# Last projection tile computed in two column halves, first loads cut in half, last row factor by Ln and Exp

## The reference

```
def rmsnorm(x, g):
    y = xf * lax.rsqrt(jnp.mean(xf * xf, axis=-1, keepdims=True) + RMS_EPS)
    return (y * g.astype(jnp.float32)).astype(x.dtype)

h = x
for layer in range(2):
    xn = rmsnorm(h, norm_mix_g[layer])
    # layer 0: xn @ w_in (1024 x 2048), S5 and mLSTM groups, @ w_out
    # layer 1: xn @ w_qkv, windowed attention, @ w_o
    h = h + mix
    # gated MLP: up (1024 x 5632), conv of width 3, silu, times value, down (2816 x 1024)
    h = h + conv_gated_mlp(rmsnorm(h, norm_ffn_g[layer]), ...)
return rmsnorm(h, norm_final_g)
```

## Time and profile before

| | us |
|---|---|
| median of 3 runs | 1170.82 |
| lowest, highest | 1168.13, 1171.21 |
| profiled execution, its own time | 1169.44 |
| profiled execution, span from first to last instruction | 1167.6 |
| PE busy in the span | 1108.7 (95%) |
| DVE, ACT, POOL busy | 666.2, 460.8, 200.6 |
| mean granted TensorE clock | 0.976 |

### The profile page before, as it was taken

The page is one execution under the profiler, slowest core; times in us unless marked ns, Lnnn a source line. Parts: engine busy times, 40 slices in busy tenths (PEclk is TensorE's granted clock), DMA queues, the critical chain, the costliest instruction groups (busy, mean ns, idle before and its releaser), DMA issues.

```text
span 1167.6 us, 15374 instructions
## 1 busy us (share of the span) xinstructions
PE 1108.7 (95%) x5472; PEld 885.9 (76%) x5472; DVE 666.2 (57%) x870; ACT 460.8 (39%) x667; POOL 200.6 (17%) x310
## 2 busy tenths in 40 slices
PE   8978867999999999999999999999999999999995
PEld 7857533787888888888888777777888888888883
DVE  5875846365766666663333576358666666642223
ACT  6224322445444444432223356345444444422221
POOL 8972992012000000000000021121000000000011
PEclk9988978999999999999999999999999999999998
DMA  6622110132322322323323311133223223232321
GB/s 229 129 87 73 38 58 0 51 131 91 105 94 90 108 90 91 107 90 108 108 96 102 118 42 50 37 104 102 101 90 105 92 91 107 90 108 96 103 72 72
DMA packets 34169, 106.70 MB, mean 91 GB/s; under 512 B 7568, under 2 KB 7824, under 8 KB 34000
## 3 DMA queue, kind: packets, MB, share of 16 engines
q1 hardware_dynamic: 34128, 106.15, 28.2%
HBM read 101.55 MB, written 3.15 MB: 90 GB/s over the span
## 4 chain that ended last, share of the span: by engine, by line
PE 76%; DVE 2%; ACT 2%; issue 1%; POOL 0%; DVEq 0%; ACTq 0%; POOLq 0%
PE bank L1326 24%; PE bank L1328 24%; PE bank L1327 23%; PE bank L1620 1%; PE bank L1349 1%; PE bank L1642 1%; ACT whi L617 1%; DVE h L1160 1%; PE bank L1486 0%; ACT sq L623 0%; DVE xlo L901 0%; POOL ssum L417 0%; DVE outb L1315 0%; DVE rstd L907 0%; PE bank L1346 0%
## 5 line engine op out<-in xcount | busy, mean ns | idle before, releaser
L1326 PE MATMUL bank<-xhi,whi 128*128 128x512 f32 x992 | 392.5, 396 | 9.6 <-DVE wlo L895 3.1
L1327 PE MATMUL bank<-xlo,whi 128*128 128x512 f32 x992 | 387.9, 391 | 0.0
L1328 PE MATMUL bank<-xhi,wlo 128*128 128x512 f32 x992 | 387.6, 391 | 0.0
L895 DVE TENSOR_TENSOR wlo<-raw,whi 128x1024 fp32r<-128x1024 f32 x181 | 226.7, 1253 | 277.7 <-ACT whi L617 276.8
L617 ACT ACTIVATE whi<-raw 128x1024 fp32r<-128x1024 f32 x181 | 191.3, 1058 | 383.1 <-PE bank L1328 345.9
L1326 PEld LDWEIGHTS bank<-xhi,whi 128*128 128x128 f32 x992 | 187.3, 189 | 54.1 <-DVE wlo L895 6.5
L1328 PEld LDWEIGHTS bank<-xhi,wlo 128*128 128x128 f32 x992 | 187.3, 189 | 39.4
L1327 PEld LDWEIGHTS bank<-xlo,whi 128*128 128x128 f32 x992 | 187.4, 189 | 39.1 <-issue 1.0
L1326 PE MATMUL bank<-ahi,whi 128*128 128x512 f32 x352 | 138.7, 394 | 0.0
L1328 PE MATMUL bank<-ahi,wlo 128*128 128x512 f32 x352 | 138.0, 392 | 0.0
L1327 PE MATMUL bank<-alo,whi 128*128 128x512 f32 x352 | 136.6, 388 | 0.0
(11 more groups left out here) (229 smaller groups left out, 1104.6 us busy)
## 6 DMA issues: line engine op xcount, KB each, us to landing
raw<-wstream SPq DMA_DIRECT2D x181, 512.0 KB, 3.3
xin<-xT SPq DMA_DIRECT2D x4, 512.0 KB, 7.1
h<-xT SPq DMA_DIRECT2D x1, 2048.0 KB, 7.5
outT<-outb SPq DMA_DIRECT2D x8, 256.0 KB, 2.2
u_scratch<-uperm SPq DMA_DIRECT2D x1, 1024.0 KB, 5.0
uc<-u_scratch SPq DMA_DIRECT2D x8, 128.0 KB, 5.3
bcp<-bc SPq DMA_DIRECT2D x1, 512.0 KB, 4.8
bandsb<-band SPq DMA_DIRECT2D x1, 512.0 KB, 3.3
```

The lines of the kernel that those rows point to most:

```text
L895: V.tensor_tensor(wlo[:, t % RING, :], raw[:, t % RAWS, :], whi[:, t % RING, :].bitcast(f32), ALU.subtract).then_inc(lo_done, 1)
L1326: MM(dst, wh, rhi, start=start, stop=False)
L1327: MM(dst, wh, rlo, start=False, stop=False)
L1328: return MM(dst, wl, rhi, start=False, stop=stop)
```

## The change

Three edits, and what they need:

- **Halves at the end.** The eighth down tile is computed as tokens 0 to 255 in one bank and tokens 256 to 511 in bank 4, each with all 22 blocks of weights: 132 matmuls of 256 columns in place of 66 of 512. Add, square, mean, factor, output and stores go by halves as well. The mean matmuls of the first half stand between the first and the second weight tile of the second half. `outb` moves to where `xhi` was, since it is now written while `ahi` is still read. The loop of the last down projection on PE is written out.
- **Last factor.** In place of Sqrt on ACT and reciprocal on DVE, ACT computes exp(-0.5 * ln(mean + eps)) in two instructions for each half, with one table load for both functions, ahead of the first Ln. DVE alone writes the output, 16 pieces of 256 columns; POOL's two blocks and ACT's scaling of `h` for them go. A store carries two blocks of one half, 256 KB as before.
- **Half-size first pieces.** x comes in eight pieces of 256 KB, the first four weight tiles in eight halves of 512 columns. The gain of the first norm (8 columns of `prm`) is loaded ahead of all, the rest of `prm` after the first x block and the first half tile. ACT and DVE alternate: one block of x, one half tile. PE's first product needs block 0 and half a tile.

How the instructions move, in their order on each engine. First PE at the end of the program: the last block of the eighth tile before, the loop's branch, and the two mean matmuls (ssum is POOL's sum, sq ACT's last square).

One block of x and half a tile stand where two blocks and a whole tile stood. The diff, cut to what the prediction speaks of:

```diff
-    outb = at("outb", [P, KB, SEQ], base)
+    outb = at("outb", [P, KB, SEQ], xn_at)
...
-        sp.dma_start(prm[:, 0:NCOL], params).then_inc(params_in, 16)
-        for k in range(4):
-            sp.dma_start(xin[:, 2 * k:2 * k + 2, :], xT[:, 2 * k:2 * k + 2, :]).then_inc(x_in[k], 16)
-            if k in (0, 1):
-                sp.dma_start(raw[:, k, :], wstream[k]).then_inc(raw_in[k], 16)
+        sp.dma_start(prm[:, 0:KB], params[:, 0:KB]).then_inc(gain_in, 16)
+        for k in range(KB):
+            sp.dma_start(xin[:, k, :], xT[:, k, :]).then_inc(x_in[k], 16)
+            if k < 4:
+                part = slice(512 * (k % 2), 512 * (k % 2) + 512)
+                sp.dma_start(raw[:, k // 2, part], wstream[k // 2][:, part]).then_inc(
+                    raw_in[k // 2] if k % 2 else half_in[k // 2], 16)
+            if k == 0:
+                sp.dma_start(prm[:, KB:NCOL], params[:, KB:NCOL]).then_inc(params_in, 16)
+        for t in (2, 3):
+            for k in range(2):
+                part = slice(512 * k, 512 * k + 512)
+                if k:
+                    sp.wait_ge(lo_done, t - 1)
+                else:
+                    sp.wait_ge(half_lo, t - 1)
+                sp.dma_start(raw[:, t % RAWS, part], wstream[t][:, part]).then_inc(
+                    raw_in[t % RAWS] if k else half_in[t], 16)
...
-        for m in STORES:
-            if m < POOL_OUT:
-                sp.wait_ge(pool_out, m + 1)
-            else:
-                sp.wait_ge(out_done, m - POOL_OUT + 1)
-            sp.dma_start(outT[:, m, :], outb[:, m, :]).then_inc(out_saved, 16)
-        sp.wait_ge(out_saved, 16 * KB)
+        for k in range(8):
+            part, ms = HALF[k // 4], slice(2 * (k % 4), 2 * (k % 4) + 2)
+            sp.wait_ge(out_done, 2 * k + 2)
+            sp.dma_start(outT[:, ms, part], outb[:, ms, part]).then_inc(out_saved, 16)
+        sp.wait_ge(out_saved, 16 * 8)
...
-        pool.wait_ge(hg_done, POOL_OUT)
-        pool.wait_ge(rstd_done, 5)
-        for m in range(POOL_OUT):
-            G.tensor_tensor(outb[:, m, :], h[:, m, :], rstd[:, :], ALU.mult).then_inc(pool_out, 1)
...
+        def last_factor():
+            act.wait_ge(out_freed, O_DN[1])
+            for hf in range(2):
+                act.wait_ge(half_added, hf + 1)
+                if hf == 0:
+                    act.wait_ge(acc_done, 5 * KB - 2)
+                A(sq[:, (KB - 1) % 2, HALF[hf]], h[:, KB - 1, HALF[hf]], ACT.Square).then_inc(half_squared, 1)
+                if hf == 0:
+                    act.preload_act_table_set("natural_log_exp_and_others")
+                act.wait_ge(half_mean, hf + 1)
+                A(rstd[:, HALF[hf]], bank[7 - hf][:, HALF[hf]], ACT.Ln, bias=prm[:, NCOL:NCOL + 1]).then_inc(half_log, 1)
+                act.wait_ge(half_log, hf + 1)
+                A(rstd[:, HALF[hf]], rstd[:, HALF[hf]], ACT.Exp, scale=-0.5).then_inc(half_factor, 1)
...
+        act.wait_ge(gain_in, 16)
+        for k in range(KB):
+            act.wait_ge(x_in[k], 16)
+            A(xhi[:, k, :], xin[:, k, :], ACT.Copy, scale=col("g_mix0", k)).then_inc(xhi_done, 1)
+            t, part = k // 2, slice(512 * (k % 2), 512 * (k % 2) + 512)
+            act.wait_ge(raw_in[t % RAWS] if k % 2 else half_in[t], 16 * (t // RAWS + 1) if k % 2 else 16)
+            A(whi[:, t, part], raw[:, t % RAWS, part], ACT.Copy).then_inc(hi_done if k % 2 else half_hi, 1)
+            if k == 0:
+                act.wait_ge(params_in, 16)
+                A(sm[:, 39, :], cols("ldt"), ACT.Exp).then_inc(dt_done, 1)
...
-        root_mean_square(4)
+        last_factor()
...
+        dve.wait_ge(gain_in, 16)
+        for k in range(KB):
+            dve.wait_ge(x_in[k], 16)
+            dve.wait_ge(xhi_done, k + 1)
+            V.scalar_tensor_tensor(out=xlo[:, k, :], in0=xin[:, k, :], scalar=col("g_mix0", k),
+                                   in1=xhi[:, k, :].bitcast(f32), op0=ALU.mult,
+                                   op1=ALU.subtract).then_inc(xlo_done, 1)
+            t, part = k // 2, slice(512 * (k % 2), 512 * (k % 2) + 512)
+            dve.wait_ge(hi_done if k % 2 else half_hi, t + 1)
+            V.tensor_tensor(wlo[:, t, part], raw[:, t % RAWS, part], whi[:, t, part].bitcast(f32),
+                            ALU.subtract).then_inc(lo_done if k % 2 else half_lo, 1)
...
-        row_factor(4)
-        for m in range(POOL_OUT, KB):
-            V.scalar_tensor_tensor(out=outb[:, m, :], in0=h[:, m, :], scalar=col("g_fin", m), in1=rstd[:, :],
-                                   op0=ALU.mult, op1=ALU.mult).then_inc(out_done, 1)
+
+        def add_half(hf):
+            dve.wait_ge(half_ready, hf + 1)
+            V.tensor_tensor(h[:, KB - 1, HALF[hf]], h[:, KB - 1, HALF[hf]], last_bank[hf][:, HALF[hf]],
+                            ALU.add).then_inc(half_added, 1)
+
+        def scale_half(hf, ms):
+            dve.wait_ge(half_factor, hf + 1)
+            for m in ms:
+                V.scalar_tensor_tensor(out=outb[:, m, HALF[hf]], in0=h[:, m, HALF[hf]], scalar=col("g_fin", m),
+                                       in1=rstd[:, HALF[hf]], op0=ALU.mult, op1=ALU.mult).then_inc(out_done, 1)
+
+        add_half(0)
+        dve.wait_ge(half_added, 1)
+        scale_half(0, range(0, 4))
+        add_half(1)
+        scale_half(0, range(4, KB))
+        dve.wait_ge(half_added, 2)
+        scale_half(1, range(0, KB))
...
-            pe.wait_ge(lo_done, t + 1)
             for b in (2 * t, 2 * t + 1):
                 pe.wait_ge(xlo_done, b + 1)
+                pe.wait_ge(lo_done if b % 2 else half_lo, t + 1)
...
+            for m in range(KB - 1):
+                down(m // 4, m % 4)
+            pe.wait_ge(out_freed, O_DN[1] + KB - 4)
+            for hf in range(2):
+                for part, ks in enumerate(parts):
+                    t = T_DN[1] + 3 * (KB - 1) + part
+                    if hf == 0:
+                        pe.wait_ge(lo_done, t + 1)
+                    for k in ks:
+                        ins = block3(last_bank[hf][:, HALF[hf]], t % RING, k - ks[0], ahi[:, k, HALF[hf]],
+                                     alo[:, k, HALF[hf]], k == 0, k == FJ - 1)
+                    if hf == 1 and part == 0:
+                        last_mean(0)
+                ins.then_inc(half_ready, 1)
+            last_mean(1)
+
+        def last_mean(hf):
+            if hf == 0:
+                pe.wait_ge(acc_done, KB * 5 - 1)
+                pe.wait_ge(rms_done, 4)
+            MM(bank[7 - hf][:, HALF[hf]], mean_w[:, :], ssum[:, HALF[hf]], start=True, stop=False)
+            pe.wait_ge(half_squared, hf + 1)
+            MM(bank[7 - hf][:, HALF[hf]], mean_w[:, :], sq[:, (KB - 1) % 2, HALF[hf]], start=False,
+               stop=True).then_inc(half_mean, 1)
...
-        pe.wait_ge(acc_done, KB * 5 - 1)
-        MM(bank[7][:, :], mean_w[:, :], ssum[:, :], start=True, stop=False)
-        pe.wait_ge(sq_done, KB * 5)
-        MM(bank[7][:, :], mean_w[:, :], sq[:, (KB - 1) % 2, :], start=False, stop=True).then_inc(mean_done, 1)
```

More of the change, by code:

```diff
@@ L254, in build @@
     params_in, con_in, bc_in, band_in = sem("params_in"), sem("con_in"), sem("bc_in"), sem("band_in")
-    x_in = [sem(f"x_in{k}") for k in range(4)]
+    x_in = [sem(f"x_in{k}") for k in range(KB)]
     consts_set = sem("consts_set")
@@ L817, in down @@
                         split_hi(d0 + s + RING, i, 12)
-                    if s % 3 == 2:
+                    if s % 3 == 2 and not (last and s == 11):
                         m = s // 3
-                        if last and s == 11:
-                            for k in range(POOL_OUT):
-                                A(h[:, k, :], h[:, k, :], ACT.Copy, scale=col("g_fin", k)).then_inc(hg_done, 1)
                         act.wait_ge(out_freed, i * 4 + (O_DN[l] + m + 1))
@@ L1207, in down @@
             def down(i, last):
-                for s in range(12):
+                for s in range(8 if last else 12):
                     wait_tile_used(dve, (d0 + s, i, 12))
```

62 lines of the change are left out of this document (28 added, 34 removed).

## The result

The changed kernel took 1160.97 us, the median of five runs (1160.52 to 1164.26), against 1170.47 for the kernel before (five runs, 1168.10 to 1171.21). The ratio is 0.9934, with a 95% interval of 0.9914 to 0.9954. My forecast was 1160.5, so the total is where I had put it. The sum behind it isn't: the end gave more than forecast, and the start much less. The two medians also flatter the change. With six runs more of the changed kernel, and all the runs of before beside every comparison, the means are 1162.07 (11 runs) and 1169.21 (60 runs). That is 7.1 us apart, plus or minus 1.1 (two standard errors).

The account below looks back on a forecast made before the run. PE ends the longest chain for 76% of the span, so gains lie where it stands still, at both ends. End -5.7 and start -3.8 gave 1159.9; half of a 1.4 run offset made 1160.5, range 1157.0 to 1167.5.

Parts of the forecast that it names:

- The narrow matmul: Last down tile: 132 matmuls of 256 columns at 0.12 us each, 15.8 in all, 0.7 more than before.
- The rivals at 0.188 and 0.295 per matmul: Last tile: recorded load sets the pace, 1169.5 us, chance 0.06; or load not hidden at all, 1183.6, chance 0.06.
- The chain at the end: From the second half's feed to the span's end: 9.2 us against 16.5; net of 1.6 later feed, -5.7.
- Both covers: Last tile: first factor ready 3.8 us before second half is fed; four remaining pieces hidden before second factor, 0.7 spare.
- The start: Half-size first pieces end the first tiles at 30.3 us against 34.1: -3.8, bounds 0 and -5.
- First product at 6.5: Program start: PE's first product at 6.5 us instead of 9.48, possibly 5.9 or 7.2.
- the clock stays at 2.4 GHz: PE's first stream: the gap after the warm-up matmuls closes, so no slow matmuls; 1.5 us gained.
- They may begin about 1 earlier, so PE waits 0.9: First norm: squares start about 1 us earlier than 17.10, so PE waits 0.9 at the mean, due at 23.0.
- 12 us of slack, so no: POOL's `g_built` at 74, PE asking at 86.4: 12 us of slack, so the start's gain isn't given back.
- moves along: PE's wait for DVE near 90 us shifts with the first tiles' banks, to 86.4 from 90.23.
- The sum: Whole kernel: -5.7 at the end and -3.8 at the start make -9.5 us, forecast 1160.5.
- start's gain is taken back: Rival: before 90 us, a late POOL coefficient or shared bandwidth takes back the start's 3.8; 1164.3 us, chance 0.14.

Follow-up runs that it names:

- e11: The changed kernel with the seventh tile of the last projection in four quarters of 128 columns, 264 matmuls in place of 66; 1176.93 us in a single execution.
- e2: The kernel before with the half-size first pieces alone, its end as before; 1168.19 us (12 runs), ratio 0.9989.
- e10: The changed kernel once more, unchanged, as a measure of scatter; 1161.96 us (6 runs), ratio 0.9942.
- e6: The changed kernel with the first norm's mean product moved on PE into the fourth weight tile, behind its first 12 matmuls; 1159.64 us (6 runs), ratio 0.9925.

## Why the prediction was right, and where it was wrong

**The narrow matmul**: right. 0.12 taken, 0.117 measured; +0.4 for the tile in place of +0.7. The row that decided, 128 columns of fp32 at 0.11 under a full load, was the right one: e11 has 0.112. The rivals at 0.188 and 0.295 per matmul had no part in the result.

**The chain at the end**: 9.2 forecast, 8.7 measured. The pieces are 0.41 apart, not 0.36 (3.26 in place of 3.0), but from the last piece to the end are 2.5 us, not 3.2 with up to 1 more for short runs. In all -6.5 (-6.5 to -6.6 in the table's last column) against -5.7. Both covers held: the first factor is there at 1146.3, 3.9 before the second half is added; 0.68 is left ahead of the second.

**The start**: wrong, and this is the step that failed. "First product at 6.5" (6.64) and "the clock stays at 2.4 GHz" in the first stretch were right. Three things were not.

- "They may begin about 1 earlier, so PE waits 0.9": the squares began 1.5 later. I had followed the first block through the smaller pieces, and not the other seven. ACT waited 0.93 for the parameters, 1.00 for the second x block and 1.97 for the third weight tile (1.57 before), in front of the squares in its queue. Its first piece came 1.5 sooner, but from there to the squares it stood still for 4.3 in place of 2.3 and worked for 10.2 in place of 9.2, since two half pieces cost it more than a whole one (0.63 each against 1.06 for `whi`) and the parameters' Exp of 0.2 now stands there too. PE's wait was 2.0 to 2.4 in five profiles with this start, 2.6 and 3.2 in two more.
- Behind that wait the clock fell to 1.2 GHz for 3.4 us in three of the seven (changed kernel, e2, e11) and in four not, the one with the longest wait, 3.2, among them. Each time it cost 1.7. I had given the clock to the start as a gain and not as a risk at the next stop. With these two, the first profile adds up: PE at the mean product 3.35 sooner, less 2.19 of waiting, less 1.7 of clock, is `uperm` 0.5 later. In e10, without the slow stretch, it is 3.7 less 2.2, and `uperm` 1.45 sooner.
- "12 us of slack, so no", the gain isn't given back, and PE's wait "moves along" with the first banks: it doesn't move one for one. Of e10's 1.45 at `uperm`, 0.4 are left at `gg`, of e6's 2.7 there are 1.7. I had looked for a coefficient of POOL that comes late for PE, and not at what DVE's queue itself meets on the way: POOL's large steps beside its convolutions, and transfers that don't come sooner. The 12 us were also counted from the end of PE's wait, 90.23; PE had asked at 83.4.

**The sum**: -9.5 forecast. The medians of the first five runs are 9.5 apart, the means of the same runs 7.7, the two profiled spans 8.9, and the means of all runs 7.1, which is 6.5 at the end and 0.6 to 0.8 ahead of it. So the start gave 3.0 less than forecast and the end 0.8 more, and the 2.4 between the forecast and the means were made up by the scatter of the first runs: that the total was hit was luck. The first profile had some too, 1.7 between `gg` and the seventh add, in the stretch with the higher clock. The rival "start's gain is taken back" (1164.3) names what happened to that part; with the end's real size it would have said 1163.5. The mean of the changed kernel's runs, 1162.07, lies between that and my 1160.5.

## What to carry to other kernels

Before a faster start or feed is priced, look at the first instruction of the engine whose queue sets the next stretch, and follow each of its operands back to the point where the faster engine has to wait for another. Here that was the mean product: PE could be 2.6 sooner (27.46 against 24.85) before the squares' sum would hold it up, and the change itself made that sum 1.4 later. Follow every piece of a finer split through the queues, not only the first. At the end of a program, where one chain is all that is left, split the last tile as narrow as the weight load covers, and put the part that is ready under the part that isn't: that was worth 2.5 us, and the end as a whole could be summed to within 1 us from durations in the trace.

## What the runs showed of the hardware

- A weight load of 128 columns is recorded as 0.19 us, and loads under a stream of short matmuls follow one another every 0.112 (e11). The record isn't the pace. The Trainium skill (TensorE: Matmul & The Clock Gate, section LDWEIGHTS), cited in the prediction, has a formula that gives 107 ns for 128 columns, and the trace agrees within 5%. The sentence of the Trainium skill (same page, section The mechanism) that a load overlaps running matmuls only when it goes to another row group would give 0.295 here and is not borne out by any run; the same section also names a background weight buffer as a target for which loads are pulled ahead, which these traces would fit.
- A reciprocal on DVE cost nearly in proportion to its columns: 3.35 for 512, 1.75 for 256. Ln and Exp on ACT cost 0.69 and 0.63 for 512, 0.47 and 0.42 for 256.
- POOL and DVE at work side by side: the same three DVE instructions took 2.37 beside small steps of POOL and 3.70 beside its large ones, and the tensor-scalar ahead of them 0.55 and 1.36. The Trainium skill (SBUF — State Buffer, section SBUF: two separate sides) describes a port pair that VectorE, for instance with two SBUF inputs, or GpSimd holds for a whole instruction while the other waits; the trace agrees in kind for DVE. For POOL it is open: its last large step ended at 75.3 in e6, and at 73.9 and 74.6 in the two profiles of the changed kernel.
- Behind a PE wait of 2.2 to 2.6 us in the stream the granted clock fell to 0.50 for 3.4 us in three executions, and behind waits of 2.0, 2.1, 2.2 and 3.2 it stayed at 1.00 in four. The length of the wait alone doesn't decide it.
- The clock in a stretch with many short waits differs between executions, 0.85 to 0.93 over 52 us, and with it 2 us of the time; the changed kernel's own two profiles have 0.93 and 0.92. What decides it stays open.
